# Attention probabilities: a 32x32 block transpose through device memory in place of TensorE transposes, ScalarE scaling, and the product with the values 512 columns later

## The reference

```python
def one_block(qblk):
    sc = jnp.einsum('blkrd,bskd->bkrls', qblk, k).astype(jnp.float32)
    prob = jax.nn.softmax(sc, axis=-1).astype(v.dtype)
    return jnp.einsum('bkrls,bskd->blkrd', prob, v)
...
branch_a = y_ssm @ w_ssm_up[layer]
branch_b = y_attn @ w_attn_up[layer]
```

## Time and profile before

| | |
|---|---|
| Time, median of 3 runs | 1609.04 us (1609.0 to 1609.05) |
| The profiled execution: its own time | 1609.39 us |
| Its span in the trace | 1607.3 us |
| Granted TensorE clock | 0.998 of full speed |
| TensorE busy | 1595.4 us (99% of the span) |
| VectorE busy | 1278.8 us (80%) |
| ScalarE busy | 928.0 us (58%) |
| GpSimd busy | 79.2 us (5%) |

### The profile page before, as it was taken

One profiled execution on the slowest core, in us unless ns is written; L12 is line 12 of the kernel. 1 busy time (PEld: TensorE's weight loads), 2 busy tenths in 40 slices (PEclk: granted clock), 3 DMA queues, 4 the chain that ended last, 5 costly groups with the idle time before them and its releaser, 6 DMA issues.

```text
span 1607.3 us, 20614 instructions
## 1 busy us (share of the span) xinstructions
PE 1595.4 (99%) x7984; PEld 1349.2 (84%) x7984; DVE 1278.8 (80%) x1521; ACT 928.0 (58%) x1264; POOL 79.2 (5%) x67
## 2 busy tenths in 40 slices
PE   9999999999999999999999999999999999999998
PEld 7888888888888888888888888888888888888886
DVE  7978877888767688876666667999899988998893
ACT  7665566665666545554445555665566655655562
POOL 3000000000000134000000000000000000000000
PEclk9999999999999999999999999999999999999999
DMA  7665656665688776545877875558645863686461
GB/s 272 202 201 184 201 183 211 197 198 185 196 244 238 231 225 200 172 145 181 244 265 235 278 228 178 181 171 266 188 133 200 275 192 123 204 281 214 143 244 53
DMA packets 144993, 327.93 MB, mean 204 GB/s; under 512 B 10944, under 2 KB 19328, under 8 KB 144768
## 3 DMA queue, kind: packets, MB, share of 16 engines
q1 hardware_dynamic: 129376, 302.21, 58.5%
q10 hardware_dynamic: 15520, 24.41, 5.2%
HBM read 316.55 MB, written 10.03 MB: 203 GB/s over the span
## 4 chain that ended last, share of the span: by engine, by line
PE 95%; DVE 2%; issue 1%; DMA 1%; ACT 0%; POOL 0%; POOLq 0%; SPq 0%; ACTq 0%
PE G L1835 17%; PE G L1836 17%; PE G L1837 17%; PE G L1844 13%; PE S L1844 7%; PE G L1848 6%; PE S L1835 4%; PE S L1836 4%; PE S L1837 4%; PE S L1848 4%; PE S L1962 1%; DMA raw<-in_w_in 1%; DVE wlo L1108 1%; PE S L1990 0%; PE S L1939 0%
## 5 line engine op out<-in xcount | busy, mean ns | idle before, releaser
L668 ACT ACTIVATE whi<-raw 128x1024 fp32r<-128x1024 f32 x395 | 416.6, 1059 | 396.4 <-PE G L1837 230.4
L1108 DVE TENSOR_TENSOR wlo<-raw,whi 128x1024 fp32r<-128x1024 f32 x395 | 483.3, 1238 | 132.1 <-ACT whi L668 130.5
L1835 PE MATMUL G<-whi,a_both 128*128 128x512 f32 x768 | 300.0, 391 | 2.5 <-DVE wlo L1108 2.0
L1837 PE MATMUL G<-whi,a_both 128*128 128x512 f32 x768 | 299.0, 389 | 0.0
L1836 PE MATMUL G<-wlo,a_both 128*128 128x512 f32 x768 | 299.0, 389 | 0.0
L1844 PE MATMUL G<-a_both,whi 128*128 128x512 f32 x640 | 201.5, 396 | 0.0
L1835 PEld LDWEIGHTS G<-whi,a_both 128*128 128x128 f32 x768 | 144.2, 188 | 34.0 <-issue 2.8
L1837 PEld LDWEIGHTS G<-whi,a_both 128*128 128x128 f32 x768 | 144.2, 188 | 30.2
L1836 PEld LDWEIGHTS G<-wlo,a_both 128*128 128x128 f32 x768 | 144.2, 188 | 28.9
L1848 PEld LDWEIGHTS G<-a_both,wlo 128*128 128x128 f32 x640 | 120.2, 188 | 28.3
L1835 PE MATMUL G<-whi,b_hi 128*128 128x512 f32 x342 | 133.5, 390 | 0.0
(11 more groups left out here) (313 smaller groups left out, 2689.1 us busy)
## 6 DMA issues: line engine op xcount, KB each, us to landing
raw<-in_w_in SPq DMA_DIRECT2D x208, 512.0 KB, 4.4
raw<-in_w_mlp_in SPq DMA_DIRECT2D x74, 512.0 KB, 4.6
raw<-in_w_mlp_out SPq DMA_DIRECT2D x74, 512.0 KB, 4.9
gates<-in_w_mlp_in SPq DMA_DIRECT2D x54, 512.0 KB, 4.2
gates<-in_w_mlp_out SPq DMA_DIRECT2D x54, 512.0 KB, 4.8
raw<-in_w_ssm_up SPq DMA_DIRECT2D x32, 512.0 KB, 3.8
raw<-in_w_attn_up SPq DMA_DIRECT2D x32, 512.0 KB, 4.5
raw<-in_w_out SPq DMA_DIRECT2D x32, 512.0 KB, 5.2
```

Of the source, the lines that this page charges most:

```text
L668: act.activation(high(m), piece(n), ACT.Copy).then_inc(hi_made, 1)
L1108: dve.tensor_tensor(low(m), piece(n), high(m).bitcast(F32), ALU.subtract).then_inc(lo_made, 1)
L1835: pe.matmul(out_ap, hi[:, k, cols], w_hi, start=start, stop=False)
L1837: return pe.matmul(out_ap, lo[:, k, cols], w_hi, start=False, stop=stop)
```

## The change

- The four identity transposes of each head go, and with them `turn`, `copy_pt` and their semaphores. `prob` is laid out token block first, so that two heads of one token block lie side by side.
- ScalarE scales the probabilities (`normalise` on ScalarE, two activations a head, at steps 1 to 4, behind the next head's `exps`); VectorE keeps the reciprocal.
- VectorE transposes each pair of heads in 32x32 blocks (`turn_prob`, two instructions of 128x512, at steps 3 and 5). ScalarE's queue writes the result to device memory (`put_prob`, one DMA of 512 KB, at steps 4 and 7), and reads it back with the blocks in their new places (`get_prob`, four DMAs of 128 KB; for the first pair at step 6, for the second at step 1 of the next window).
- A new side `weighed` does the rest one window later, ahead of the next group's `attend` in the list: ScalarE rounds a pair at once (`high_pt`, 128x1024, steps 2 and 4), VectorE makes its remainder (`low_pt`, 128x1024, same steps), TensorE weighs two heads in a row (after pieces 3 and 5), `high` and `low` follow at steps 3 and 5. The last group is weighed in (15,0), whose pieces 6 and 7 multiply its result.
- In (13,0) `rope` stands ahead of `attend` now. Buffers move to places that are free then: the turned blocks and the read-back tiles lie in parts of the input `a` and in `tmp_b`, `pT_hi` in `tmp_a`.

```diff
@@ -87,11 +87,11 @@
     window(11, 1, "q", 1, [("rope", 1)])
     window(12, 0, "q", 2, [("heads_in", 1), ("rope", 2)])
     window(12, 1, "q", 3, [("heads_in", 2), ("rope", 3)])
-    window(13, 0, "ssm_up", 0, [("heads_in", 3), ("attend", 0), ("rope", 4)])
-    window(13, 1, "ssm_up", 1, [("heads_in", 4), ("attend", 1), ("gated_a", 0)])
-    window(14, 0, "ssm_up", 2, [("attend", 2), ("gated_a", 1)])
-    window(14, 1, "ssm_up", 3, [("attend", 3), ("gated_a", 2)])
-    window(15, 0, "attn_up", 0, [("gated_a", 3)])
+    window(13, 0, "ssm_up", 0, [("heads_in", 3), ("rope", 4), ("attend", 0)])
+    window(13, 1, "ssm_up", 1, [("weighed", 0), ("heads_in", 4), ("attend", 1), ("gated_a", 0)])
+    window(14, 0, "ssm_up", 2, [("weighed", 1), ("attend", 2), ("gated_a", 1)])
+    window(14, 1, "ssm_up", 3, [("weighed", 2), ("attend", 3), ("gated_a", 2)])
+    window(15, 0, "attn_up", 0, [("weighed", 3), ("gated_a", 3)])
     window(15, 1, "attn_up", 1, [("merged", 0)])
     window(16, 0, "attn_up", 2, [("merged", 1)])
     window(16, 1, "attn_up", 3, [("merged", 2)])
...
@@ -952,31 +963,70 @@
             def exps(h):
                 act.wait_ge(at_max, 8 * g + 2 * h + 2)
                 if g:
-                    act.wait_ge(at_t, 4 * (g - 1) + h + 1)
-                for tb in range(TB):
-                    act.activation(prob[:, h, tb, :], S[:, h % 2, tb * T:(tb + 1) * T], ACT.Exp,
+                    act.wait_ge(at_turned, 2 * (g - 1) + h // 2 + 1)
+                for tb in range(TB):
+                    act.activation(prob[:, tb, h, :], S[:, h % 2, tb * T:(tb + 1) * T], ACT.Exp,
                                    bias=nb[:, h, tb:tb + 1], scale=SCALE,
                                    accum_out=den[:, h, tb:tb + 1]).then_inc(at_exp, 1)
 
-            def copy_pt(h):
-                act.wait_ge(at_t, 4 * g + h + 1)
-                if 4 * g + h:
-                    act.wait_ge(at_pv, 4 * g + h)
-                act.activation(pT_hi[:, :, :].rearrange("p s l -> p (s l)"), S[:, 2, :], ACT.Copy
-                               ).then_inc(at_pt, 1)
+            def put_prob(pair):
+                act.wait_ge(at_turned, 2 * g + pair + 1)
+                act.dma_start(prob_rows[2 * g + pair],
+                              prob_blocks[pair][:, :, :, :, :].rearrange("p j c b t -> p (j c b t)")
+                              ).then_inc(at_put[pair], 16)
+
+            def normalise(h):
+                act.wait_ge(at_v, 4 * g + h + 1)
+                for tb in range(TB):
+                    act.activation(prob[:, tb, h, :], prob[:, tb, h, :], ACT.Copy,
+                                   scale=rden[:, h, tb:tb + 1]).then_inc(at_norm, 1)
+
+            if p < 4:
+                exps(p)
+            if 1 <= p < 5:
+                normalise(p - 1)
+            if p == 4:
+                put_prob(0)
+            if p == 6:
+                if g:
+                    act.wait_ge(at_pt_lo, 2 * g - 1)
+                get_prob(g, 0)
+            if p == 7:
+                put_prob(1)
+
+        def get_prob(g, pair):
+
+            act.wait_ge(at_put[pair], 16 * (g + 1))
+            rows = prob_rows[2 * g + pair].rearrange("(i w) (j x) -> j w i x", i=4, j=4)
+            for j in range(4):
+                act.dma_start(prob_in[pair][Q * j:Q * (j + 1), :, :, :, :].rearrange("w i c b t -> w i (c b t)"),
+                              rows[j]).then_inc(at_got[pair], 16)
+
+        def weighed(p, g, pr, pp):
+            def high_pt(pair):
+                act.wait_ge(at_got[pair], 64 * (g + 1))
+                if 2 * g + pair:
+                    act.wait_ge(at_pv, 4 * g + 2 * pair)
+                act.activation(by_block(pT_hi, 0, 4), prob_wide[pair], ACT.Copy).then_inc(at_pt, 1)
 
             def high(pair):
                 act.wait_ge(at_pv, 4 * g + 2 * pair + 2)
                 act.activation(a_hi[:, 4 * g + 2 * pair:4 * g + 2 * pair + 2, :],
                                S[:, 3, :].rearrange("p (c t) -> p c t", c=2), ACT.Copy).then_inc(at_hi, 1)
 
-            if 3 <= p < 7:
-                copy_pt(p - 3)
+            if p == 1:
+                if g:
+                    act.wait_ge(at_pt_lo, 2 * g)
+                else:
+                    act.wait_ge(r_lo, 4)
+                get_prob(g, 1)
+            if p == 2:
+                high_pt(0)
+            if p == 3:
+                high(0)
+            if p == 4:
+                high_pt(1)
             if p == 5:
-                high(0)
-            if p < 4:
-                exps(p)
-            if p == 7:
                 high(1)
 
         def gate(p, i, pr, pp):
...
@@ -1492,16 +1542,33 @@
             def normalise(h):
                 dve.wait_ge(at_exp, 8 * g + 2 * h + 2)
                 dve.reciprocal(rden[:, h, :], den[:, h, :]).then_inc(at_v, 1)
-                dve.wait_ge(at_v, (4 * g + h) * AT_V + 1)
-                for tb in range(TB):
-                    dve.tensor_scalar(prob[:, h, tb, :], prob[:, h, tb, :], rden[:, h, tb:tb + 1], None,
-                                      ALU.mult).then_inc(at_v, 1)
-
-            def low_pt(h):
-                dve.wait_ge(at_pt, 4 * g + h + 1)
-                dve.tensor_tensor(pT_lo[:, :, :].rearrange("p s l -> p (s l)"), S[:, 2, :],
-                                  pT_hi[:, :, :].rearrange("p s l -> p (s l)").bitcast(F32), ALU.subtract
-                                  ).then_inc(at_pt_lo, 1)
+
+            def turn_prob(pair):
+                dve.wait_ge(at_norm, 2 * (4 * g + 2 * pair + 2))
+                if g:
+                    dve.wait_ge(at_put[pair], 16 * g)
+                elif pair:
+                    dve.wait_ge(r_v, 5 * ROPE_V)
+                for tb in range(TB):
+                    last = dve.transpose(
+                        prob_blocks[pair][:, :, :, tb, :].rearrange("p j c t -> p c j t"),
+                        prob[:, tb, 2 * pair:2 * pair + 2, :].rearrange("p h (s j w) -> p (h s) j w", s=TB, w=Q))
+                last.then_inc(at_turned, 1)
+
+            if p < 4:
+                biggest(p)
+            if 1 <= p < 5:
+                normalise(p - 1)
+            if p == 3:
+                turn_prob(0)
+            if p == 5:
+                turn_prob(1)
+
+        def weighed(p, g, pr, pp):
+            def low_pt(pair):
+                dve.wait_ge(at_pt, 2 * g + pair + 1)
+                dve.tensor_tensor(by_block(pT_lo, 0, 4), prob_wide[pair], by_block(pT_hi, 0, 4).bitcast(F32),
+                                  ALU.subtract).then_inc(at_pt_lo, 1)
 
             def low(pair):
                 dve.wait_ge(at_hi, 2 * g + pair + 1)
...
@@ -1509,15 +1576,13 @@
                 dve.tensor_tensor(a_lo[:, k:k + 2, :], S[:, 3, :].rearrange("p (c t) -> p c t", c=2),
                                   a_hi[:, k:k + 2, :].bitcast(F32), ALU.subtract).then_inc(at_lo, 1)
 
-            if p < 4:
-                biggest(p)
-            if 3 <= p < 7:
-                low_pt(p - 3)
-            if 1 <= p < 5:
-                normalise(p - 1)
+            if p == 2:
+                low_pt(0)
+            if p == 3:
+                low(0)
+            if p == 4:
+                low_pt(1)
             if p == 5:
-                low(0)
-            if p == 7:
                 low(1)
 
         def gated(slot, pr, pp):
...
@@ -1974,39 +2039,34 @@
                 pe.wait_ge(r_lo, g + 2)
                 if (g, h) == (0, 0):
                     pe.wait_ge(scan_v, SCAN_V * GROUPS)
-                if h >= 2:
+                if g or h >= 2:
                     pe.wait_ge(at_exp, 8 * g + 2 * (h - 1))
                 for tb in range(TB):
                     last = three_passes(S[:, h % 2, tb * T:(tb + 1) * T], 4 * g + h, tb, qT_hi, qT_lo,
                                         kT_hi[:, g, :], kT_lo[:, g, :], True, True)
                 last.then_inc(at_sc, 1)
 
-            def turn(h):
-                pe.wait_ge(at_v, (4 * g + h + 1) * AT_V)
-                if 4 * g + h:
-                    pe.wait_ge(at_pt_lo, 4 * g + h)
-                for sb in range(TB):
-                    for tb in range(TB):
-                        last = pe.transpose(S[:, 2, sb * T + tb * P:sb * T + (tb + 1) * P],
-                                            prob[:, h, tb, sb * P:(sb + 1) * P], ident[:, :])
-                last.then_inc(at_t, 1)
-
+            if p < 4:
+                scores(p)
+
+        def weighed(p, g, pr, pp):
             def weigh(h):
-                pe.wait_ge(at_pt_lo, 4 * g + h + 1)
+                pe.wait_ge(at_pt_lo, 2 * g + h // 2 + 1)
                 pe.wait_ge(vg_made, 2 * g + 2)
                 if 2 * g + h // 2:
                     pe.wait_ge(at_lo, 2 * g + h // 2)
                 for sb in range(TB):
+                    part = h % 2 * TB + sb
                     last = three_passes(S[:, 3, h % 2 * T:(h % 2 + 1) * T], sb, 0, vg_hi, vg_lo,
-                                        pT_hi[:, sb, :], pT_lo[:, sb, :], sb == 0, sb == TB - 1)
```

(46 more changed lines are left out.)

## The result

The kernel after the change takes 1617.48 us (median, 1615.86 to 1617.72) beside 1609.05 us (1609.00 to 1609.82) for the one before. Run against run the ratio is 1.0044, with a 95% interval of 1.0032 to 1.0056: slower. The forecast was 1610.8, with a range up to 1613.5, and slower had a chance of 0.20. The profiled execution took 1615.86 us with a span of 1614.1 us, against a span of 1607.3 before: 6.8 us more. Two of the executions of the kernel before that ran beside the first experiments took 3260.59 and 4154.02 us, at a granted clock of 1.0, and are left out of every comparison.

A forecast was written before the change was run, and what follows sets the result against it. TensorE was taken as the bound, busy 1595.4 of 1607.3 us. 1609.4 - 7.6 for removed work + 9.4 for waits in three windows gave 1611.1 profiled, 1610.8 median; range 1607.5 to 1613.5.

The forecast's parts named there:

- What goes, -7.6: On TensorE: 16 groups of four transposes, 7.0 us, and 0.6 us of late last weighing in (13,0), all on the path.
- The chain, 3.0 us in front of heads 2 and 3: In (13,1), (14,0), (14,1): three linked rounds through ScalarE's queue make TensorE wait 3.0 us after piece 5.
- The scaling's 0.80: ScalarE's scaling of probabilities takes 0.40 per activation, 0.80 us a head, and is in the chain three times.
- With 0.1 us for the restart: TensorE's matmuls after the wait at heads 2 and 3 cost 0.1 us extra: 3.1 a window, 9.4 in three.
- ScalarE doesn't wait for writes ahead of `exps(1)`: Sign: ScalarE's queue, where pair 1's read stands ahead of `exps(1)`, is not held by a write still landing.
- second rival: Late device memory writes hold ScalarE's queue, 2 x 1.1 us more in each of three windows: 1617.4 us; chance 0.10.
- L: Landing time of a `put_prob` write; 24.0 + 2L + 2 x 1.8 must stay below 38.8, so it decides from 5.6.
- no such wait: (13,0) and (15,0) have only one half of the chain, so TensorE has no wait of that kind there.
- The margin of 1.1 ahead of piece 7: In (15,0), piece 6 (2.74 us) hides the last group's `high` and `low`, with about 1.1 us to spare.
- SP's weight loads aren't moved: Listed under what costs nothing by itself: weight loads issued by SP keep their places.
- GpSimd beside VectorE, taken as nothing: GpSimd's splitting beside `low` and block transposes in step 5 costs between nothing and 0.5 us a window; nothing was taken.

The follow-up runs named there:

- the chain is taken apart: Changed kernel with `weighed` last, `high_pt(0)` and `low_pt(0)` earlier, second pair's read behind `exps(1)`, heads 2 and 3 weighed one piece later; 1603.15 us.
- Filling the gap: Twelve unused matmuls of 512 columns before weighing heads 2 and 3 in three windows, added to the changed kernel with pair 1's read behind `high_pt(0)`; 1611.5 us.

## Why the prediction was wrong

The chain, its place in front of heads 2 and 3 and its size were right; the sum left out what comes behind a wait, and two waits in front of heads 0 and 1. In the order of the forecast's steps:

- **What goes, -7.6.** Held: 0.43 a head again with the transposes doubled, and -7.3 us by medians once the chain is taken apart.
- **The chain, 3.0 us in front of heads 2 and 3.** Held in (14,0) and (14,1), 2.89 each. The scaling's 0.80 held. That the ordering makes it, not memory, is shown from both sides: it stays without memory and goes with the order. In (13,1) it was cut to 1.41 by the wait before it.
- **"With 0.1 us for the restart" is the step that failed.** I took from the earlier trace rows that TensorE starts again at once at its pace, but there it had stood for 0.45 us, and the earlier trace rows have no longer wait. After waits of 2.48 and 2.73 us it ran at half clock, after another of 2.73 not: 3.1 us in place of 0.3. Filling the gap shows this cost by itself. The trace of before has no wait longer than 1.5 us, so nothing there bounded it at 0.1; it should have been an open cost with an upper end.
- **"ScalarE doesn't wait for writes ahead of `exps(1)`" was wrong in (13,1).** The second rival's inequality was near enough, at L = 5.6, and it was set aside by the median. It takes one L for two writes; the write of group 0's second pair goes out right behind `rope`'s and landed after 7.0, the first pair's after 4.5. The window's waits and a restart sum to 4.1 us where 3.1 was forecast: +1.0. The rival had asked for this in each of three windows and was wrong in that.
- **(15,0) "no such wait" was wrong.** The margin of 1.1 ahead of piece 7 held: TensorE's list has no wait there. The wait came earlier, in front of heads 0 and 1, because the weight loads came late, and 1.0 us was lost. "SP's weight loads aren't moved" is true and not enough: in that stretch their median time to land doubled. Without the writes and reads TensorE has no wait there, and the loads land after a median of 5.4 in place of 8.2. The traffic of that window alone was not taken away, so that it delays the loads is likely and not shown.
- **GpSimd beside VectorE, taken as nothing.** Held: TensorE never waits for `wlo` in these windows.
- **The size of the miss.** The sum itself is rounded a little (3 x 3.1 is 9.3, not 9.4), which changes nothing. In the profiled execution 1615.86 - 1611.1 = 4.8 us: 3.1 of half clock, 1.0 in (13,1), 1.0 in (15,0), and -0.3 because the chain was shorter than 3.0 + 0.1 in the other two. The other executions took 1.5 to 1.9 us more. More half clock doesn't explain that: their granted clocks are 0.997, 0.996 and 0.996, beside 0.996 for the profiled one. What does stays open, since no trace has it.

## What to carry to other kernels

When two chains share in-order queues, write down for each wait what stands behind it: a side placed first in the list is harmless until its wait is the late one. If TensorE is the bound, a wait of two to four microseconds is to be charged above its length, for the clock behind it (1.4 to 2.8 us here, most times); and when a wait is removed, ask whose time it was giving. Work through device memory was nearly free here once the order was right, but a read that stands on a computing engine's queue behind its own write makes that engine wait for that write's own landing, 7.0 us here, not for the median.

## What the runs showed of the hardware that was not expected

- Two waits of the same 2.73 us had different consequences: granted clock 0.55 over the 2.9 us after one and 1.00 after the other. Both came behind long stretches in which TensorE was busy; what tells them apart wasn't found. Over all twelve profiles TensorE has 13 single waits of 2.3 to 4.3 us, and a stretch at 0.50 came with 11 of them; none came with any wait of up to 1.5 us.
- 36 matmuls more, without use, made a kernel 5.0 us faster (1616.47 to 1611.5), with the granted clock at 0.998 or 0.999 in place of 0.995 to 0.997.
- Writes of 512 KB beside the weight loads landed after 2.6 to 7.0 us, and after up to 9.8 with the weighing one piece later.
